# Decay and rate products of an RWKV-7 head pair issued as three groups with alternating row halves instead of eight single products

## The chip, the cores and the metric

One core of a Trainium2 chip runs the whole kernel. The metric is device time in microseconds, the median over runs of the whole program. Engines: PE (TensorE, matmul), DVE (VectorE), ACT (ScalarE), POOL (GpSimd), SP (SyncE, DMA issue). Matmul results land in PSUM, which has eight banks; one bank holds 512 fp32 columns of 128 partitions. All matmuls here are fp32, and each shows as two instructions in the trace.

## The reference, cut to what matters

The model has two layers over 768 tokens (256 context, 512 latent) with model width 1024. Each layer holds a bidirectional RWKV-7 time mixing, a conformer convolution, a gated MLP, a merge and a SwiGLU. The change lies in the first. Per layer, for each of the two directions d, the reference computes

```python
lw = (w0[d] + jnp.tanh(z[..., ow:ow + DECAY_LORA]) @ w_up[d])      # DECAY_LORA = 64
decay = jnp.exp(-jnp.exp(-jax.nn.softplus(-lw) - 0.5))
a = jax.nn.sigmoid(a0[d] + z[..., oa:oa + ICLR_LORA] @ a_up[d])    # ICLR_LORA = 64
k_d = kf * (1.0 + (a - 1.0) * k_a)
S = S * w_t - (S kk_t) kka_t^T + v_t k_t^T                         # the scan over tokens, per head
```

with `kk = k * k_k`, divided by its norm over each head (the norm squared is floored). The two products with `w_up[d]` and `a_up[d]` contract over 64, half of PE's 128 rows.

## The kernel before

**Staging.** `pair_phase(l)` handles layer l in turns t = 0 to 9; turns 0 to 7 each start one pair of heads (KT = 8 pairs, 128 of the 1024 channels each). In turn t PE issues `dense(t)`, the projections of pair t, woven with `scan(t-1)`, the chunked delta rule of the pair before, and with side work. The order is written by hand: `WEAVE["PE", l, t]` is a string in which d takes the next step of `dense`, s the next of `scan` and x the next of the side work. Strings ("A", l, t) and ("V", l, t) do the same for ACT and DVE, where p is a step of the pair's preparation (`rest`). Semaphores between engines are wrapped as events; each `wait_ge` holds up everything behind it on its engine.

**The scan of a pair** has, among other work, 16 bursts of 48 matmuls in 32x32 tiles per turn (96 instructions in the trace, L1156). Between bursts DVE masks a product (L2617, event t_masked), subtracts one (L2622, u_taken) and transposes it (L2601, x_turned); the next burst of that chain waits for it. Two chains, h0 and h1, alternate. Below, um3h0 is the burst that yields chain h0's u-product at level 3, um3h1 the same of chain h1, and tm4h0 the next burst of chain h0, whose product DVE masks for level 4. In layer 0 with t = 3 they start at 615.54, 619.45 and 622.08 us in the profile.

**The dense part.** k, r and v of a pair each take 8 accumulating matmuls per half of the tokens (`k_tiles`, `r_tiles`, `v_tiles`; L1040): the latent half (512 columns) lands in bank 0, the context half (256 columns) in bank 1. Between them stand single products (`single()`, L1052): four decay products and four rate products (64 rows deep; direction 0 in the upper 64 rows, direction 1 in the lower), and the two norm sums of kk², `norm_tile(t, 0)` and `norm_tile(t, 1)`, 128 rows deep. Both norm sums land in bank 0 (`LANDS["kkn"]`). Before any product starts in a bank, `hold` makes PE wait for the reader of the bank's last tenant:

```python
def hold(b, reader):
    if b in held:
        pe.wait_ge(*held[b])
    held[b] = reader
```

The reader of a k or r result is ACT's copy (L1806, L1807; raw_k, raw_r), of a decay product ACT's sigmoid `decay_gate` (L1858), of a rate product `rate_gate` (L1869), and of a norm sum DVE's `norm_max` (L2446, kk_max). DVE's queue of a turn has, in `rest`, the token shifts of k and r (L2394, L2398), two scans over 768 tokens (L2491) that wait for all four decay gates, a subtraction (L2495), then `norm_max(0)` and `norm_max(1)`.

**Tables.** `tables(n)` on ACT loads the function table n if another is loaded (ACT_TABLE_LOAD, L1701).

## Time and profile before

| what | before |
|---|---|
| median of 3 runs | 4074.63 us (4072.68 to 4075.27) |
| profiled execution, its own time | 4079.55 us |
| its span in the profile | 4077.7 us |
| PE busy | 3880.4 us, 95% |
| DVE busy | 1687.0 us, 41% |
| ACT busy | 1146.1 us, 28% |
| POOL busy | 551.5 us, 14% |
| mean granted clock of PE | 0.986 |

The span is the profile's stretch from first to last instruction. The profiled execution is one more run, 4.9 us longer than the median of the three. Busy shares are means over stages with different limits.

### The profile page before, as it was taken

To read this page: it belongs to the slowest core of one execution; us is meant where nothing else is said; L and a number is where in the kernel's file an instruction comes from. 1 tells how busy PE (TensorE), PEld (TensorE's weight loads), DVE (VectorE), ACT (ScalarE), POOL (GpSimd) and SP (SyncE) were. 2 spreads that over 40 slices of the span, in tenths; PEclk is the share of its full clock that TensorE was granted. 3 is DMA by queue.
4 is the path that set the end of the run, shared out by engine and by line. 5 is a ranking of instruction groups with operands and counts; after the bars stand their busy time and mean duration, and the time that the engine had idled before them with its cause. 6 is when DMAs were issued, how large, how long until landed. Compare 5 with 4: busy or idle time off the path is not lost.

```text
span 4077.7 us, 111806 instructions
## 1 busy us (share of the span) xinstructions
PE 3880.4 (95%) x51352; PEld 2546.8 (62%) x51352; DVE 1687.0 (41%) x2721; ACT 1146.1 (28%) x2003; POOL 551.5 (14%) x436
## 2 busy tenths in 40 slices
PE   7899999999999999999999988999998999999998
PEld 3566666666555555655555556666666556678887
DVE  2555566664862111322231254555555422122232
ACT  3444444442122000200000344444444221021001
POOL 0000000000032221122232000000000023213443
PEclk8999999999999999999999999999999999999999
DMA  5000000000333223211112300000010253242224
GB/s 205 25 9 24 25 25 25 25 22 28 108 131 104 93 88 95 79 61 62 52 62 73 123 25 9 23 23 23 23 34 21 68 194 114 83 144 92 85 89 129
DMA packets 76337, 277.40 MB, mean 68 GB/s; under 512 B 8672, under 2 KB 13024, under 8 KB 75488
## 3 DMA queue, kind: packets, MB, share of 16 engines
q1 hardware_dynamic: 67968, 235.96, 18.1%
q10 hardware_dynamic: 6624, 29.04, 1.9%
q8 instruction: 408, 6.68, 0.7%
q0 software_dynamic: 1280, 5.24, 0.3%
q14 instruction: 57, 0.47, 0.0%
HBM read 256.58 MB, written 13.63 MB: 66 GB/s over the span
## 4 chain that ended last, share of the span: by engine, by line
PE 90%; ACT 4%; issue 3%; DVE 2%; DMA 1%; POOL 0%; ACTq 0%; DVEq 0%; SPq 0%; POOLq 0%
PE psum L1156 17%; PE psum L1670 16%; PE psum L1040 12%; PE psum L741 11%; PE psum L1467 9%; PE psum L1602 6%; PE psum L1052 5%; PE psum L1562 3%; PE psum L1625 2%; PE psum L1188 2%; PE psum L732 2%; PE psum L1000 2%; DMA ring<-w_stream_in 1%; PE psum L1018 1%; PE psum L921 1%
## 5 line engine op out<-in xcount | busy, mean ns | idle before, releaser
L1156 PEld LDWEIGHTS psum<-arena 32*32 32x32 f32 (+3 forms) x40512 | 697.6, 117 | 375.4 <-issue 301.4
L1156 PE MATMUL psum<-arena 32*32 32x32 f32 (+4 forms) x40512 | 790.8, 208 | 105.4 <-issue 73.7
L1040 PE MATMUL psum<-arena,ring 128*128 128x512 f32 (+1 forms) x1408 | 573.1, 523 | 2.5 <-ACT arena L1858 1.6
L741 PE MATMUL psum<-arena,ring 128*128 128x512 f32 (+1 forms) x1264 | 463.1, 524 | 3.8 <-DVE arena L2552 3.8
L741 PEld LDWEIGHTS psum<-arena,ring 128*128 128x128 f32 x1264 | 238.8, 191 | 230.3 <-issue 200.7
L1670 PE MATMUL psum<-arena 128*128 128x384 f32 (+1 forms) x1344 | 368.6, 433 | 0.0
L1040 PEld LDWEIGHTS psum<-arena,ring 128*128 128x128 f32 x1408 | 239.2, 191 | 142.0 <-issue 115.5
L1670 PEld LDWEIGHTS psum<-arena 128*128 128x128 f32 x1344 | 255.4, 190 | 106.4
L2991 POOL DMA_DIRECT2D ya_spill<-arena x16 | 8.8, 550 | 1995.2 <-DVE arena L2552 1995.2
L1670 PE MATMUL psum<-arena,ring 128*128 128x384 f32 (+1 forms) x1008 | 278.5, 433 | 0.0
L1670 PEld LDWEIGHTS psum<-arena,ring 128*128 128x128 f32 x1008 | 191.6, 190 | 79.5
L2834 DVE TENSOR_TENSOR arena<-psum,arena 128x384 f32<-128x384 f32 (+1 forms) x210 | 99.2, 489 | 309.9 <-PE psum L1670 309.9
L1467 PE MATMUL psum<-arena 128*128 128x384 f32 (+1 forms) x768 | 215.9, 434 | 3.0 <-POOL arena L3028 1.8
L1701 ACT ACT_TABLE_LOAD x106 | 136.0, 1283 | 191.2 <-PE psum L1052 83.2
L1467 PEld LDWEIGHTS psum<-arena 128*128 128x128 f32 x768 | 145.9, 191 | 66.6 <-issue 4.0
L1467 PE MATMUL psum<-arena,ring 128*128 128x384 f32 (+1 forms) x576 | 169.1, 437 | 14.5 <-DMA ring<-w_stream_in 8.2
L2376 DVE TENSOR_TENSOR arena<-arena 128x768 f32<-128x768 f32 x192 | 175.2, 930 | 11.5 <-ACT arena L1930 6.6
L2359 DVE SCALAR_TENSOR_TENSOR arena<-arena,par 128x255 f32<-128x255 f32 (+18 forms) x296 | 166.3, 596 | 5.3
L2723 DVE TENSOR_TENSOR arena<-psum,arena 128x384 f32<-128x384 f32 (+1 forms) x120 | 56.6, 488 | 252.0 <-PE psum L1467 251.9
L1467 PEld LDWEIGHTS psum<-arena,ring 128*128 128x128 f32 x576 | 108.3, 191 | 67.9 <-issue 6.5
L1052 PE MATMUL psum<-arena 64*128 64x512 f32 (+3 forms) x304 | 140.9, 544 | 7.1 <-ACT arena L1807 2.3
L1602 PE MATMUL psum<-arena 128*128 128x384 f32 (+1 forms) x528 | 145.1, 433 | 0.0
(175 smaller groups left out, 4428.6 us busy)
## 6 DMA issues: line engine op xcount, KB each, us to landing
ring<-w_stream_in SPq DMA_DIRECT2D x440, 512.0 KB, 3.8
x_spill<-arena ACTq DMA_DIRECT2D x2, 3072.0 KB, 8.7
arena<-x_spill ACTq DMA_DIRECT2D x16, 384.0 KB, 6.5
arena<-ya_spill ACTq DMA_DIRECT2D x6, 768.0 KB, 6.0
ring<-w_stream_in ACTq DMA_DIRECT2D x8, 512.0 KB, 6.4
arena<-x_in ACTq DMA_DIRECT2D x1, 3072.0 KB, 14.3
arena<-ups_in SPq DMA_DIRECT2D x16, 192.0 KB, 2.4
ya_spill<-arena POOLq DMA_DIRECT2D x8, 384.0 KB, 6.3
```

The costliest lines, as they stand in the source:

```text
L741: mm = eng.matmul(psum[0:lhs[k].shape[-1], tile, a - off:b - off], lhsT=lhs[k], rhs=rhs[k][:, a:b], start=(k == 0), stop=(k == len(lhs) - ...
L1040: mm = pe.matmul(bank(j, z=b - a), lhsT=w[k], rhs=hs[k][:, a:b], start=(k == 0), stop=(k == KT - 1))
L1052: pe.matmul(bank(b, z=z - a), lhsT=lhs, rhs=rhs[:, a:z], start=True, stop=True).then_inc(ev.sem, 2 if skip else 1)
L1156: return pe.matmul(out, lhsT=lhs, rhs=rhs, start=start, stop=stop, skip_group_check=True)
L1467: mm = pe.matmul(bank(FREE_BANK[i], z=m), lhsT=left[:, k * P:k * P + P], rhs=right[:, k], start=(k == 0 and i != 2), stop=(k == 3), skip_g ...
L1562: mm = pe.matmul(psum[:, tile, a - c0:b - c0], lhsT=w, rhs=mov[k][:, a:b], start=(k == 0), stop=(k == len(mov) - 1), skip_group_check=True)
L1602: mm = pe.matmul(bank(DOWN_BANK[i], z=m), lhsT=left[:, k * P:k * P + P], rhs=right[:, k], start=((p, i) not in begun and k == 0), stop=(c ...
L1670: mm = pe.matmul(bank(b, z=m), lhsT=left[:, k * P:k * P + P], rhs=right[:, k], start=(k == 0 and i != 2), stop=(k == 3), skip_group_check= ...
L1701: act.add_instruction(mybir.InstLoadActFuncSet(name=nc.get_next_instruction_name(), engine=act.engine, act_func_set_id=n))
L2359: return dve.scalar_tensor_tensor(out=out, in0=in0, scalar=w, in1=out, op0=ALU.mult, op1=ALU.add)
L2376: dve.tensor_tensor(out, a, b, ALU.mult).then_inc(ev.sem, 1)
L2834: dve.tensor_tensor(out, x, y, op).then_inc(*V.mark(name))
```

## The change

1. The eight single decay and rate products of a turn become three groups (`up_group`), each of eight matmuls with 64 rows and 128 columns that take direction 0 (upper rows) and direction 1 (lower rows) by turns, into bank 0 for direction 0 and bank 1 for direction 1 (in turn 0 banks 2 to 7). Group "first" is decay of the latent half, "both" is decay and rate of the context half, "last" is rate of the latent half. In `dense`, "first" follows the k tiles, "both" the latent r tiles, "last" the context r tiles. Each is one letter of the weave.
2. Both norm products move earlier among the context r tiles, and the weave strings of turns 1 to 7 are rewritten.
3. ACT's order in `rest` follows; on DVE `r_shift(0)` moves ahead of the two scans; one weave string of DVE changes by one letter.
4. Everywhere `tables(...)` is called ahead of the wait instead of behind it.

```diff
-UP_ORDER = ((0, 0), (1, 1), (1, 0), (0, 1))
+UP_ORDER = dict(lw=((0, 0), (1, 0), (1, 1), (0, 1)), la=((1, 1), (0, 1), (0, 0), (1, 0)))
+UP_GROUPS = dict(first=(("lw", 0, 0),), both=(("lw", 1, 0), ("la", 1, 256)), last=(("la", 0, 0),))
+UP_BANK = dict(first=2, both=4, last=6)
-LANDS = dict(mean=(1, 1), bonus=(1, 0), lw=(0, 0, 0, 1), la=(1, 1, 0, 0), kkn=(0, 0), var=(1, 1), gu=(0, 0))
+LANDS = dict(mean=(1, 1), bonus=(1, 0), kkn=(0, 0), var=(1, 1), gu=(0, 0))
...
+        def up_bank(t, group, d):
+            return d + (0 if t else UP_BANK[group])
...
-                def up_tile(t, name, ev, src, n, reader, j):
-                    if t < KT:
-                        g = KT * l + t
-                        d, half = UP_ORDER[j]
...
-                        yield from single(name, ev, g, j, half, ups_block(g, n, side(d)), slot(src)[side(d)], reader.at(g, j), True)
...
+                def up_group(t, group):
...
+                    name, half, at = UP_GROUPS[group][-1]
+                    for d in DIRS:
+                        hold(up_bank(t, group, d), (sw if name == "lw" else sa).at(g, UP_ORDER[name].index((d, half))))
+                    for name, half, at in UP_GROUPS[group]:
...
+                        for c in range(a, b, P):
+                            for d, h in UP_ORDER[name]:
+                                if h != half:
+                                    continue
+                                mm = pe.matmul(bank(up_bank(t, group, d), a=at + c - a, z=at + c - a + P), lhsT=ups_block(g, n, side(d)),
+                                               rhs=slot(src, c, c + P)[side(d)], start=True, stop=True, skip_group_check=True)
+                                if c + P == b:
+                                    mm.then_inc(ev.sem, 1)
+                    yield
...
-                    yield from decay_tile(t, 0)
                     yield from k_tiles(t, 1, 4, 6)
-                    yield from decay_tile(t, 1)
                     yield from k_tiles(t, 1, 6, 8)
-                    yield from decay_tile(t, 2)
+                    yield from up_group(t, "first")
                     yield from r_tiles(t, 0, 0, 2)
-                    yield from decay_tile(t, 3)
                     yield from r_tiles(t, 0, 2, 4)
-                    yield from rate_tile(t, 0)
                     yield from r_tiles(t, 0, 4, 6)
-                    yield from rate_tile(t, 1)
                     yield from r_tiles(t, 0, 6, 8)
+                    yield from up_group(t, "both")
                     yield from r_tiles(t, 1, 0, 2)
-                    yield from rate_tile(t, 2)
-                    yield from r_tiles(t, 1, 2, 4)
-                    yield from rate_tile(t, 3)
                     yield from norm_tile(t, 0)
-                    yield from r_tiles(t, 1, 4, 6)
+                    yield from r_tiles(t, 1, 2, 6)
                     yield from norm_tile(t, 1)
                     yield from r_tiles(t, 1, 6, 8)
+                    yield from up_group(t, "last")
...
                     yield from k_shift(1)
+                    yield from r_shift(0)
                     if prep:
                         for d in DIRS:
                             dve.wait_ge(*sw.at(g, 3))
...
-                    yield from r_shift(0)
                     yield from norm_max(0)
```

In PE's queue of layer 0, turn t=3, before, the stretch from the burst of chain h1 at level 3 to the second norm product reads as follows. L1156 rows are bursts, L1040 rows are r tiles, L1052 with 64 rows deep are rate products, and the two L1052 rows that wait for kk_square are the norm products.

```order
653 L1156 MATMUL psum<-arena 32x32 [waits x_turned]
654 L1156 MATMUL psum<-arena 32x32 x47
655 L1040 MATMUL psum<-arena,ring 128x256 x2
656 L1052 MATMUL psum<-arena 128x256 [waits rate_gate,ups_in_0]
657 L1156 MATMUL psum<-arena 32x32 [waits x_turned]
658 L1156 MATMUL psum<-arena 32x32 x47
659 L1052 MATMUL psum<-arena,const 128x512 [waits rate_gate,kk_square]
660 L1040 MATMUL psum<-arena,ring 128x256 x2
661 L1156 MATMUL psum<-arena 32x32 [waits t_masked]
662 L1156 MATMUL psum<-arena 32x32 x47
663 L1052 MATMUL psum<-arena,const 128x256 [waits kk_max,kk_square]
```

After the change the same engine and place, with the line numbers of the new program (L1173 bursts, L1054 r tiles, L1066 norm products, L1122 the groups; row 642 opens the group "last").

```order
631 L1066 MATMUL psum<-arena,const 128x512 [waits rate_gate,kk_square]
632 L1054 MATMUL psum<-arena,ring 128x256 x2
633 L1173 MATMUL psum<-arena 32x32 [waits x_turned]
634 L1173 MATMUL psum<-arena 32x32 x47
635 L1054 MATMUL psum<-arena,ring 128x256 x2
636 L1066 MATMUL psum<-arena,const 128x256 [waits kk_max,kk_square]
637 L1173 MATMUL psum<-arena 32x32 [waits x_turned]
638 L1173 MATMUL psum<-arena 32x32 x47
639 L1054 MATMUL psum<-arena,ring 128x256 x2
640 L1173 MATMUL psum<-arena 32x32 [waits t_masked]
641 L1173 MATMUL psum<-arena 32x32 x47
642 L1122 MATMUL psum<-arena 128x128 [waits raw_r,kk_max,ups_in_0]
```

The first norm product moved from behind both x_turned bursts to ahead of them, and the second from behind the next t_masked burst to ahead of the second x_turned burst; it still waits for kk_max, the read of the first.

In DVE's queue the same turn, before, from the subtraction for chain h0 to the read of the first norm sum, reads:

```order
254 L2622 TENSOR_TENSOR arena<-arena,psum 128x384 [waits u_product]
255 L2601 STREAM_TRANSPOSE arena<-arena 128x384 [waits u_taken]
256 L2491 SCALAR_TENSOR_TENSOR arena<-arena 128x768 [waits decay_gate] x2
257 L2622 TENSOR_TENSOR arena<-arena,psum 128x384 [waits u_product]
258 L2495 TENSOR_TENSOR arena<-arena 128x768 [waits decay_sums]
259 L2601 STREAM_TRANSPOSE arena<-arena 128x384 [waits u_taken]
260 L2617 TENSOR_TENSOR arena<-psum,const 128x384 [waits t_product]
261 L2394 SCALAR_TENSOR_TENSOR arena<-arena,par 128x511 [waits raw_r]
262 L2398 SCALAR_TENSOR_TENSOR arena<-arena,par 128x511 [waits shifted_r]
263 L2446 TENSOR_SCALAR arena<-psum 128x512 [waits kk_norm]
```

After, the same stretch, up to the first norm sum's read (L2463):

```order
254 L2639 TENSOR_TENSOR arena<-arena,psum 128x384 [waits u_product]
255 L2618 STREAM_TRANSPOSE arena<-arena 128x384 [waits u_taken]
256 L2411 SCALAR_TENSOR_TENSOR arena<-arena,par 128x511 [waits raw_r]
257 L2415 SCALAR_TENSOR_TENSOR arena<-arena,par 128x511 [waits shifted_r]
258 L2639 TENSOR_TENSOR arena<-arena,psum 128x384 [waits u_product]
259 L2509 SCALAR_TENSOR_TENSOR arena<-arena 128x768 [waits decay_gate]
260 L2618 STREAM_TRANSPOSE arena<-arena 128x384 [waits u_taken]
261 L2634 TENSOR_TENSOR arena<-psum,const 128x384 [waits t_product]
262 L2509 SCALAR_TENSOR_TENSOR arena<-arena 128x768 [waits decay_gate]
263 L2513 TENSOR_TENSOR arena<-arena 128x768 [waits decay_sums]
264 L2463 TENSOR_SCALAR arena<-psum 128x512 [waits kk_norm]
```

The two shifts of r (L2394 and L2398, now L2411 and L2415) moved from just ahead of `norm_max(0)` to ahead of the scans, and the two scans are apart by a transpose and a mask; the number of instructions between the subtraction and `norm_max(0)` is the same.

In layer 1 there are no context r tiles. PE's queue of its turn t=3 before, around the norm products (L1188 are transposes by matmul):

```order
3910 L1156 MATMUL psum<-arena 32x32 [waits x_turned]
3911 L1156 MATMUL psum<-arena 32x32 x47
3912 L1052 MATMUL psum<-arena 128x256 [waits rate_gate,ups_in_1]
3913 L1052 MATMUL psum<-arena,const 128x512 [waits rate_gate,kk_square]
3914 L1156 MATMUL psum<-arena 32x32 [waits t_masked]
3915 L1156 MATMUL psum<-arena 32x32 x47
3916 L1188 MATMUL psum<-const,arena 128x128 [waits token_major]
3917 L1188 MATMUL psum<-const,arena 128x128 x3
3918 L1052 MATMUL psum<-arena,const 128x256 [waits kk_max,kk_square]
```

And after, from the group "both" to the second norm product and the burst behind it:

```order
3835 L1122 MATMUL psum<-arena 128x128 [waits decay_gate,raw_r,ups_in_1]
3836 L1122 MATMUL psum<-arena 128x128 x7
3837 L1173 MATMUL psum<-arena 32x32 [waits t_masked]
3838 L1173 MATMUL psum<-arena 32x32 x47
3839 L1205 MATMUL psum<-const,arena 128x128 [waits token_major]
3840 L1205 MATMUL psum<-const,arena 128x128 x3
3841 L1066 MATMUL psum<-arena,const 128x512 [waits rate_gate,kk_square]
3842 L1173 MATMUL psum<-arena 32x32 [waits x_turned]
3843 L1173 MATMUL psum<-arena 32x32 x47
3844 L1066 MATMUL psum<-arena,const 128x256 [waits kk_max,kk_square]
3845 L1173 MATMUL psum<-arena 32x32 [waits x_turned]
3846 L1173 MATMUL psum<-arena 32x32 x47
```

Between the first and the second norm product stands one burst; before there were a burst and four transposes, and the first came two bursts later in the scan.

## Rows read from the trace of the kernel before

**Rows 1.** The page: busy time, the chain that ended last, and the costliest PE group.

```profile
PE 3880.4 (95%) x51352; PEld 2546.8 (62%) x51352; DVE 1687.0 (41%) x2721; ACT 1146.1 (28%) x2003; POOL 551.5 (14%) x436
...
PE 90%; ACT 4%; issue 3%; DVE 2%; DMA 1%; POOL 0%; ACTq 0%; DVEq 0%; SPq 0%; POOLq 0%
...
L1156 PE MATMUL psum<-arena 32*32 32x32 f32 (+4 forms) x40512 | 790.8, 208 | 105.4 <-issue 73.7
```

**Rows 2.** Timeline, PE, turn t=3 of layer 0: start us, length us, engine, line, operation.

```profile
595.38 1.12 PE L1052 MATMUL psum<-arena 64*128 64x512 f32 x2
596.43 0.70 PE L1040 MATMUL psum<-arena,ring 128*128 128x256 f32 x2
...
598.88 0.70 PE L1052 MATMUL psum<-arena 64*128 64x256 f32 x2
599.51 1.13 PE L1040 MATMUL psum<-arena,ring 128*128 128x256 f32 x4
```

**Rows 3.** Timeline, PE: a run of `product()` in the same row halves.

```profile
357.75 2.06 PE L1156 MATMUL psum<-arena 64*128 64x128 f32 x32
359.74 0.44 PE L1188 MATMUL psum<-const,arena 128*128 128x128 f32 x2
```

**Rows 4.** Timeline, DVE, turn t=3 of layer 0, from the product of um3h0 on.

```profile
617.24 0.55 DVE L2622 TENSOR_TENSOR arena<-arena,psum 128x384 f32<-128x384 f32 x1 [3.10 <-PE psum L1156]
...
624.63 0.75 DVE L2398 SCALAR_TENSOR_TENSOR arena<-arena,par 128x511 f32<-128x511 f32 x1
626.83 0.69 DVE L2446 TENSOR_SCALAR arena<-psum 128x512 f32<-128x512 f32 x1 [1.45 <-PE psum L1052]
```

**Rows 5.** Timeline, PE, the same stretch.

```profile
617.10 2.42 PE L1040 MATMUL psum<-arena,ring 128*128 128x512 f32 x6
...
622.08 1.02 PE L1156 MATMUL psum<-arena 32*32 32x32 f32 x96
623.03 1.13 PE L1040 MATMUL psum<-arena,ring 128*128 128x256 f32 x4
624.09 0.70 PE L1052 MATMUL psum<-arena 64*128 64x256 f32 x2
...
625.67 1.13 PE L1052 MATMUL psum<-arena,const 128*128 128x512 f32 x2
626.63 1.03 PE L1040 MATMUL psum<-arena,ring 128*128 128x256 f32 x4
627.59 1.26 PE L1156 MATMUL psum<-arena 32*32 32x32 f32 x96
```

**Rows 6.** Timeline, DVE, turn t=3 of layer 1.

```profile
2735.30 0.56 DVE L2622 TENSOR_TENSOR arena<-arena,psum 128x384 f32<-128x384 f32 x1 [2.00 <-PE psum L1156]
...
2741.86 0.75 DVE L2398 SCALAR_TENSOR_TENSOR arena<-arena,par 128x511 f32<-128x511 f32 x1
2744.04 0.69 DVE L2446 TENSOR_SCALAR arena<-psum 128x512 f32<-128x512 f32 x1 [1.44 <-PE psum L1052]
```

**Rows 7.** Timeline, ACT: a rate gate of 256 columns.

```profile
615.65 0.47 ACT L1869 ACTIVATE arena<-psum,par 128x256 f32<-128x256 f32 x1 [3.40 <-PE psum L1052]
```

**Rows 8.** Timeline, ACT: a table load in a norm between phases.

```profile
2284.87 1.28 ACT L1701 ACT_TABLE_LOAD   x1 [1.24 <-PE psum L944]
```

**Rows 9.** Timeline, PE: two idle stretches inside bursts.

```profile
392.37 0.44 PE L1156 MATMUL psum<-arena 32*32 32x32 f32 x28 [1.53 <-issue]
...
3142.23 0.39 PE L1156 MATMUL psum<-arena 32*32 32x32 f32 x25 [3.08 <-issue]
```

**Rows 10.** Windows: us, length, busy PE, PEld, DVE, ACT, POOL, granted clock, DMA share, GB/s.

```profile
376.00:488.00 112.00, 107.98 (x2746) 72.88 (x2745) 64.92 (x100) 51.26 (x92) 0.55 (x1) 0.97 0.07 23
596.00:702.00 106.00, 104.06 (x2744) 71.28 (x2743) 64.55 (x100) 51.25 (x92) 0.54 (x1) 1.00 0.08 24
...
392.90:399.70 6.80, 6.80 (x105) 3.32 (x106) 1.08 (x2) 0.69 (x1) 0.00 (x0) 0.50 0.02 5
3142.20:3149.20 7.00, 4.87 (x256) 3.10 (x255) 2.61 (x5) 0.00 (x0) 0.00 (x0) 1.00 0.02 5
```

More of the change, by code:

```diff
@@ L186 @@
 WEAVE.update((("PE", 1, t), (
-    "ddddxsdxxssxsddxdssxdxxdddddddssdddsxdxsdsxdddddssdddsddsdssdsdssdsddxddsdsxddddsddssssssddsdssssssd"
-    "sssssssdssssssssssssssssssssssssss")) for t in (1,))
+    "ddddxsdxxssxsddxdssxdxxddddddddsxsdxsddsddsxddsddsdsdssssdssdsddxddsdsxddddsddssssssddsdssssssdsssss"
+    "ssdssssssssssssssssssssssssss")) for t in (1,))
 WEAVE.update((("PE", 1, t), (
-    "xxsssdsxssxxdxxddddsxdsdxsddddsdddsdddsdddxsdsddsddsddsddsddsxdsddsxdsdsddxsddddsddsdsssddssdsssssds"
-    "ssdssssdddsssssssssssssssssssssssssss")) for t in range(2, KT))
+    "xxsssdsxssxxdxxddddsxdsdxsddddsddddsddsdxsddsddsddsddxsdsxdsdssdsdsddxsddddsddsdsssddssdsssssdsssdss"
+    "ssdddsssssssssssssssssssssssssss")) for t in range(2, KT))
 WEAVE.update((("PE", 1, t), (
@@ L645, in state_sum, with up_result @@
             return bank((6 if n < 8 else 4) + d, rows, n % 8 * C, n % 8 * C + C)
+        def up_bank(t, group, d):
+            return d + (0 if t else UP_BANK[group])
+        def up_result(t, name, j):
+            d, half = UP_ORDER[name][j]
+            group, at = [(k, at) for k, parts in UP_GROUPS.items() for n, h, at in parts if (n, h) == (name, half)][0]
+            a, b = HALVES[half]
+            return bank(up_bank(t, group, d), a=at, z=at + b - a)
         def wk(c, rows=slice(0, P), a=0, b=P):
@@ L1087, in bonus_tile @@
                         yield from single("bonus", bonus, g, j, j, heads, slot(BN + g % 2), bv.at(g, j), False)
-                def up_tile(t, name, ev, src, n, reader, j):
-                    if t < KT:
-                        g = KT * l + t
-                        d, half = UP_ORDER[j]
-                        pe.wait_ge(ups[g % 3], 16 * (g // 3 + 1))
-                        if t == 0 and j == 0:
-                            pe.wait_ge(*phases["lora"]["A"].end(l))
-                            pe.wait_ge(*phases["lora"]["V"].end(l))
-                        yield from single(name, ev, g, j, half, ups_block(g, n, side(d)), slot(src)[side(d)], reader.at(g, j), True)
-                def decay_tile(t, j):
-                    yield from up_tile(t, "lw", lw, LW, 0, sw, j)
-                def rate_tile(t, j):
-                    yield from up_tile(t, "la", la, LA, 1, sa, j)
+                def up_group(t, group):
+                    if t >= KT:
+                        return
+                    g = KT * l + t
+                    pe.wait_ge(ups[g % 3], 16 * (g // 3 + 1))
+                    if t == 0 and group == "first":
+                        pe.wait_ge(*phases["lora"]["A"].end(l))
+                        pe.wait_ge(*phases["lora"]["V"].end(l))
+                    name, half, at = UP_GROUPS[group][-1]
+                    for d in DIRS:
+                        hold(up_bank(t, group, d), (sw if name == "lw" else sa).at(g, UP_ORDER[name].index((d, half))))
+                    for name, half, at in UP_GROUPS[group]:
+                        (a, b), n, src, ev = HALVES[half], "lw la".split().index(name), LW if name == "lw" else LA, lw if name == "lw" else la
+                        for c in range(a, b, P):
[7 more added lines that the diff above has]
+                    yield
                 def norm_tile(t, j):
@@ L1854, in decay_gate @@
                                 act.wait_ge(*kq.at(g - 1, 1))
-                            d, half = UP_ORDER[j]
-                            act.wait_ge(*lw.at(g, j))
+                            d, half = UP_ORDER["lw"][j]
                             tables(SIGMOID)
-                            act.activation(slot(SW + d, *HALVES[half]), landed("lw", j, half), ACT.Sigmoid, bias=vec(f"w0{d}", t)).then_inc(sw.sem, 1)
+                            act.wait_ge(*(lw.at(g, j) if half == 0 else la.at(g, j - 2)))
+                            act.activation(slot(SW + d, *HALVES[half]), up_result(t, "lw", j), ACT.Sigmoid, bias=vec(f"w0{d}", t)).then_inc(sw.sem, 1)
                             yield
@@ L1865, in rate_gate @@
                                 act.wait_ge(*sv.at(g - 1, 3))
-                            d, half = UP_ORDER[j]
+                            d, half = UP_ORDER["la"][j]
+                            tables(SIGMOID)
                             act.wait_ge(*la.at(g, j))
-                            tables(SIGMOID)
-                            act.activation(slot(SA + d, *HALVES[half]), landed("la", j, half), ACT.Sigmoid, bias=vec(f"a0{d}", t)).then_inc(sa.sem, 1)
+                            act.activation(slot(SA + d, *HALVES[half]), up_result(t, "la", j), ACT.Sigmoid, bias=vec(f"a0{d}", t)).then_inc(sa.sem, 1)
                             yield
```

52 lines of the change are left out of this document (26 added, 26 removed).

## Prediction

> **What bounds the kernel now.** I read the page first: PE is busy 95% of the span and is 90% of the chain that ended last [rows 1]. So a microsecond of PE work removed is a microsecond of time, as long as PE does not wait where it did not before; DVE and ACT count only through what they make PE wait for. Next I read the timeline of a whole turn of a pair phase on PE and DVE. In it PE goes from burst to product to burst with no idle time but a few stretches that the profile puts down to issue, while DVE waits for PE: the burst before the subtraction at 617.24 was waited for 3.10 us, and the first norm sum 1.45 us [rows 4]. So DVE has 1.45 us in hand at the norm sum, by PE's present order. Last I read the windows for the granted clock.
>
> **What the change removes.** A single product costs from its start to the start of the next instruction 1.05 us with 512 columns (595.38 to 596.43) and 0.63 us with 256 (598.88 to 599.51) [rows 2]. A turn has four of each: 4 x 1.05 + 4 x 0.63 = 6.7 us, and 16 turns 107.5 us.
>
> **What it adds.** 24 matmuls of 64 rows and 128 columns per turn in three groups of eight, 16 instructions in the trace each. The trace shows this shape, in alternating row halves and different banks, in another place: 32 instructions from 357.75 to 359.74, 1.99 us, the drain at both ends included [rows 3]. A group is half of that, 1.0 us; three are 3.0 us, and 16 turns 48 us. If the fixed part of those 1.99 us is a larger share than I can see, a group may take 1.15 us, which makes 7 us more. The columns done side by side are what halves the time: the single products take 1.05 us for two passes of 512 columns, the groups as many columns of both directions at once. The work of the removal minus this is **-60 us** (107.5 - 48 = 59.5).
>
> **Norm products: the new wait.** The second norm product lands in the bank of the first and so waits for `norm_max(0)`, which is behind the same ten DVE instructions as before (the order listings: subtraction, transpose, two shifts, subtraction, scan, transpose, mask, scan, subtraction). PE, however, comes there much sooner.
>
> Layer 0. DVE works without a gap from 617.24 to 624.63 + 0.75 = 625.38, which is 8.14 us; with `norm_max`'s 0.69 that is 8.83 us, from 0.14 us after the end of PE's burst um3h0 at 617.10 [rows 4, 5]: 8.97 us. The order within does not change this sum, and the decay gates for which the scans wait come in time: "both" ends one burst ahead of this point, and four gates of 256 columns, 0.47 us each [rows 7], fit into the subtraction, transpose, shifts and subtraction. PE in the new order has between um3h0's end and the second norm product: two r tiles (1.06, as 623.03 to 624.09), burst um3h1 (0.95, as 622.08 to 623.03), the first norm product (0.96, 625.67 to 626.63), two r tiles (0.96), a burst (0.95), two r tiles (0.96) [rows 5]: 5.84 us. So PE stands for 8.97 - 5.84 = 3.1 us, a little less with what the first tile waits for a rate gate; I take 3.0. Behind it in PE's queue are the burst tm4h1 and everything else, so all of it is lost.
>
> Layer 1 has no r tiles of the context half. From um3h1's product DVE works from 2735.30 to 2741.86 + 0.75 = 2742.61, with `norm_max` 8.0 us [rows 6]. PE has four transposes (0.5), norm product and burst (1.9) and, because "both" is nearer here, some 0.55 us of waiting for the rate gates, together 3.0 us. PE stands 5.0 us.
>
> In turn 0 there is no scan work on DVE between, and I count half. Sum: 7.5 x 3.0 + 7.5 x 5.0 = **+60 us**. Bounds: 45 if PE loses 1 us a turn elsewhere on its way there, 70 if turn 0 waits like the others (64) and the handoffs add 0.4 us a turn (6).
>
> **Smaller waits.** After "both" four gates of 256 columns follow on ACT, 0.47 us each [rows 7]; the first tile into bank 1 needs two of them, 0.2 + 2 x 0.45 = 1.1 us, and PE brings one burst, 0.95 us: 0.15 us a turn. The group "last" waits for `norm_max(1)`, which DVE reaches one mask after the burst behind the first; PE has 1 us to spare there. Turn 0, without bursts, has more. I take **+6 us**, between 2 and 12.
>
> **Tables.** A load is ahead of the wait now. At 2284.87 ACT is idle 1.24 us and then loads for 1.28 us [rows 8], in a norm on the path between phases; there the load disappears into the idle time. The end of the kernel has the same chain once more. 2 x 1.24 = **-2.5 us**. In the pair phases the loads stand in idle time of ACT, which is busy 28% [rows 1]; nothing, and if ACT were late there the load would only be earlier.
>
> **The clock.** The turn t=1 of layer 0 takes 112 us at a mean clock of 0.97, turn t=3 106 us at 1.00, with the same number of instructions [rows 10]. In the first is a stretch of 6.8 us at 0.50, the lower level, 1.2 GHz, right behind an idle stretch of PE of 1.53 us; behind one of 3.08 us at 3142.23 the clock stays at 1.00 [rows 9, 10]. A stretch of 6.8 us at half clock costs up to 3.4 us. The new waits make 16 idle stretches of 3 to 5 us where there were none. Of two such rows one lost its clock; I take half, 8 stretches, and 2 us each, since shorter ones cost less: **+16 us**, between 0 and 16 x 3.4 = 54.
>
> The Trainium skill ("TensorE: Matmul & The Clock Gate", Part 1 on the clock gate) has PE's clock go back to the lower level when PE has stood idle, and advises against idle gaps on it. The row at 392.37 agrees with that, the one at 3142.23 does not. By the rule each of the 16 new waits is a candidate; that is the third rival below, and it speaks against the change.
>
> **Sum.** -60 + 60 + 6 - 2.5 + 16 = +19.5 us on the profiled execution's 4079.55, that is 4099. It is 4.9 us above the median of the runs; on the median, 4074.63 + 19.5 = **4094 us**.
>
> **Rivals.**
> *The waits eat the saving and the clock holds.* As in 3142.23's case. Then +3.5 us: 4078. For it: half of the rows shown. It needs both sums to be right, so the band within 0.2% (8 us, about what a measurement of this kernel can tell from no change) gets a chance of 0.14.
> *Faster: the wait lies over idle time that is there anyway.* PE has 73.7 us of idle time in its scan matmuls put down to issue [rows 1], a lack of instructions in bursts that follow one another closely. While PE stands at the norm product its queue can fill, and the bursts behind it run without such stretches. If a third of it goes, -25 us, and the clock holds: 4074.6 + 3.5 - 25 = 4053 us. It decides from -12 us on. Against it: the three removed tiles bring bursts nearer to one another elsewhere, which makes more of these stretches. Chance 0.22, 4050 to 4066.
> *The clock drops at every wait, layer 0's too.* 16 x 3.4 = 54 in place of 16: up to 4132; with 2 to 2.5 us each, 4110 to 4118. Chance 0.15.
> *The row halves don't run side by side.* Then a group takes what its instructions take one by one, 2 us, and the saving falls to 12 us: 4142 us. The run at [rows 3] speaks against it: 62 ns an instruction. Chance 0.03.
> The forecast itself, 4083 to 4110, has 0.46.
>
> **How the numbers follow.** Faster by more than 0.2%: 0.22. Within: 0.14. Slower: 0.46 + 0.15 + 0.03, with rounding 0.64. The range reaches from the upper part of the faster rival to the clock case: 4058 to 4116; below it I leave 0.1, above 0.1. The likeliest case alone: 4083 to 4110.
>
> **What the profile after would show.** Three groups of 16 instructions per turn at 1.0 us from start to next start; PE idle 3 us before the norm product with 256 columns in layer 0 and 5 us in layer 1, released by DVE's `norm_max`, about 60 us in all in the row of the norm products; `norm_max(0)` on DVE with no idle time before it, where it has 1.45 us now; ACT's two loads between phases inside idle time; more stretches with clock 0.5 behind the norm product. I would be wrong if PE reached the norm product later than I count (if bursts on the way wait for DVE, the wait only moves), if DVE did the ten instructions in a shorter time because it waits for nothing else, or if issue stretches change by more than 10 us.

## The result and the profile after

The changed kernel takes 4137.07 us (median of 4 runs, 4127.57 to 4147.18), the kernel before 4073.65 us in the same comparison (4067.53 to 4075.27). The ratio is 1.015, 95% interval 1.0132 to 1.0168: slower by some 63 us. The sign was forecast, the size (19.5 us) was not, and the time lies above the range.

The page after has these lines for those of [rows 1]: busy time of each engine, then the chain that ended last.

```profile
PE 3861.0 (93%) x51864; PEld 2595.7 (63%) x51864; DVE 1685.6 (41%) x2721; ACT 1136.4 (28%) x2003; POOL 552.4 (13%) x436
...
PE 85%; DVE 7%; ACT 4%; issue 3%; DMA 1%; POOL 0%; ACTq 0%; DVEq 0%; SPq 0%; POOLq 0%
```

PE does 19.4 us less by its busy time, in a span that is 54.2 us longer (4131.9 to 4077.7 us): its idle time went from 197.3 to 270.9 us. DVE now has 7% of the chain, where it had 2%; that share is a rough sign, since it is 4% in the kernel before with the table loads alone moved (e4 below) and 5% in a version that has none of these waits (e11). The mean granted clock fell from 0.986 to 0.971.

The groups of PE by line, after, say where it stands idle (busy us, mean ns | idle us before the group, and what ended it):

```profile
L1173 PE MATMUL psum<-arena 32*32 32x32 f32 (+4 forms) x40512 | 807.4, 211 | 101.2 <-issue 69.3 <-ACT arena L2056 9.5 <-ACT arena L2063 3.7
...
L1205 PE MATMUL psum<-const,arena 128*128 128x128 f32 x752 | 114.2, 282 | 22.1 <-ACT arena L2005 20.7 <-ACT arena L1997 1.3
...
L1066 PE MATMUL psum<-arena,const 128*128 128x512 f32 (+1 forms) x208 | 102.9, 580 | 62.0 <-DVE arena L2463 60.4 <-ACT arena L1908 1.0 <-ACT arena L1886 0.5
...
L1122 PE MATMUL psum<-arena 64*128 64x128 f32 x768 | 69.7, 331 | 10.4 <-issue 10.3
```

The norm products wait 60.4 us for `norm_max`, the transposes 20.7 us for a copy on ACT, and the groups 10.3 us for issue. The bursts' idle time put down to issue is 69.3 us, where it was 73.7 [rows 1]. All these together, less what went (a rate gate's 5.2 us and the single products' 7.1 us of before), are the 74 us by which idle time grew.

The timeline of PE in layer 0, turn t=4, answers to [rows 5]:

```profile
507.51 1.13 PE L1054 MATMUL psum<-arena,ring 128*128 128x256 f32 x4
508.57 0.62 PE L1173 MATMUL psum<-arena 32*32 32x32 f32 x48
509.75 0.61 PE L1173 MATMUL psum<-arena 32*32 32x32 f32 x48 [0.56 <-issue]
510.29 1.12 PE L1066 MATMUL psum<-arena,const 128*128 128x512 f32 x2
511.25 1.03 PE L1054 MATMUL psum<-arena,ring 128*128 128x256 f32 x4
512.21 0.84 PE L1173 MATMUL psum<-arena 32*32 32x32 f32 x74
513.60 0.38 PE L1173 MATMUL psum<-arena 32*32 32x32 f32 x22 [0.55 <-issue]
513.91 1.13 PE L1054 MATMUL psum<-arena,ring 128*128 128x256 f32 x4
518.00 1.19 PE L1066 MATMUL psum<-arena,const 128*128 128x256 f32 x2 [2.96 <-DVE arena L2463]
519.13 1.50 PE L1173 MATMUL psum<-arena 32*32 32x32 f32 x96
...
524.00 1.16 PE L1122 MATMUL psum<-arena 64*128 64x128 f32 x16
525.09 1.09 PE L1173 MATMUL psum<-arena 32*32 32x32 f32 x76
```

PE does the two r tiles from 513.91 on and then stands 2.96 us, until 518.00. DVE's rows of the same place answer to [rows 4]. `norm_max` itself no longer waits, where it had waited 1.45 us; but DVE stands 0.94 us ahead of the mask (L2634), until PE's burst at 512.21 is done.

```profile
510.41 0.55 DVE L2639 TENSOR_TENSOR arena<-arena,psum 128x384 f32<-128x384 f32 x1 [0.23 <-PE psum L1173]
...
514.04 0.56 DVE L2634 TENSOR_TENSOR arena<-psum,const 128x384 f32<-128x384 f32 x1 [0.94 <-PE psum L1173]
...
516.30 0.96 DVE L2513 TENSOR_TENSOR arena<-arena 128x768 f32<-128x768 f32 x1
517.18 0.68 DVE L2463 TENSOR_SCALAR arena<-psum 128x512 f32<-128x512 f32 x1
```

Layer 1, turn t=5, PE:

```profile
2876.45 1.98 PE L1054 MATMUL psum<-arena,ring 128*128 128x512 f32 x4
2881.89 0.63 PE L1205 MATMUL psum<-const,arena 128*128 128x128 f32 x4 [3.46 <-ACT arena L2005]
2882.45 1.41 PE L1173 MATMUL psum<-arena 32*32 32x32 f32 x96
...
2887.76 1.10 PE L1066 MATMUL psum<-arena,const 128*128 128x512 f32 x2 [0.26 <-ACT arena L1886]
2888.78 1.02 PE L1173 MATMUL psum<-arena 32*32 32x32 f32 x96
2894.81 1.19 PE L1066 MATMUL psum<-arena,const 128*128 128x256 f32 x2 [5.01 <-DVE arena L2463]
```

Two waits: 5.01 us at the norm product, as forecast, and 3.46 us before the transposes (L1205), which the prediction does not have. ACT's rows show what it did there:

```profile
2878.53 0.60 ACT L1823 ACTIVATE arena<-psum 128x512 f32<-128x512 f32 x1 [12.89 <-PE psum L1054]
...
2879.59 0.93 ACT L1908 ACTIVATE arena<-arena,par 128x768 f32<-128x768 f32 x1
2880.55 0.59 ACT L2002 ACTIVATE arena<-psum 64x512 f32<-64x512 f32 x1
2881.16 0.59 ACT L2005 ACTIVATE arena<-psum 64x512 f32<-64x512 f32 x1
```

The copy of the latent r result (L1823) waits for PE's r tiles; behind it and the square (L1908) stand the copies of the transposed operands (L2002, L2005), and PE's next transposes need the bank that L2005 reads. So PE waits for a copy that could have run many microseconds earlier.

The windows at two of the waits at the norm product, the first of them in layer 0 and the second in layer 1 (length, busy PE, PEld, DVE, ACT, POOL, granted clock, DMA share, GB/s):

```profile
517.20:524.00 6.80, 6.00 (x198) 4.42 (x198) 1.55 (x4) 0.75 (x2) 0.00 (x0) 0.50 0.02 5
2892.90:2903.10 10.20, 7.24 (x306) 6.29 (x306) 3.66 (x7) 1.25 (x3) 0.00 (x0) 0.50 0.01 3
```

The clock is at its lower level, 1.2 GHz, for 6.8 us in the first and 10.2 us in the second. Both stretches begin while PE still waits. In layer 0 the burst at 519.13 takes 1.43 us to the next start in place of 0.95.

### The profile page after: what moved, and what is told of

It reads as the page before. It is cut to its first block, busy times and chain, and to the rows that moved or that the text cites. A ratio compares the mean times of both kernels' runs of the same rounds, so it can differ in the third digit from the quotient of the medians.

```text
span 4131.9 us, 112746 instructions
## 1 busy us (share of the span) xinstructions
PE 3861.0 (93%) x51864; PEld 2595.7 (63%) x51864; DVE 1685.6 (41%) x2721; ACT 1136.4 (28%) x2003; POOL 552.4 (13%) x436
## 4 chain that ended last, share of the span: by engine, by line
PE 85%; DVE 7%; ACT 4%; issue 3%; DMA 1%; POOL 0%; ACTq 0%; DVEq 0%; SPq 0%; POOLq 0%
PE psum L1173 17%; PE psum L1687 15%; PE psum L1054 11%; PE psum L755 9%; PE psum L1484 9%; PE psum L1619 6%; PE psum L1579 3%; DVE arena L2376 3%; PE psum L1066 3%; PE psum L1642 2%; PE psum L1205 2%; PE psum L1014 2%; PE psum L746 2%; PE psum L1122 2%; PE psum L1032 1%
## 5 line engine op out<-in xcount | busy, mean ns | idle before, releaser
L1173 PEld LDWEIGHTS psum<-arena 32*32 32x32 f32 (+3 forms) x40512 | 715.0, 121 | 352.6 <-issue 270.5
L1173 PE MATMUL psum<-arena 32*32 32x32 f32 (+4 forms) x40512 | 807.4, 211 | 101.2 <-issue 69.3
L1054 PE MATMUL psum<-arena,ring 128*128 128x512 f32 (+1 forms) x1408 | 570.1, 528 | 2.5 <-ACT arena L1824 1.3
L755 PEld LDWEIGHTS psum<-arena,ring 128*128 128x128 f32 x1264 | 238.8, 191 | 230.4 <-issue 200.9
L1687 PE MATMUL psum<-arena 128*128 128x384 f32 (+1 forms) x1344 | 368.6, 432 | 0.0
L1054 PEld LDWEIGHTS psum<-arena,ring 128*128 128x128 f32 x1408 | 246.9, 194 | 132.4 <-issue 105.1
L1687 PEld LDWEIGHTS psum<-arena,ring 128*128 128x128 f32 x1008 | 191.5, 190 | 79.6
L1484 PE MATMUL psum<-arena 128*128 128x384 f32 (+1 forms) x768 | 216.0, 435 | 2.7 <-POOL arena L3045 1.8
L1484 PE MATMUL psum<-arena,ring 128*128 128x384 f32 (+1 forms) x576 | 170.0, 439 | 13.7 <-DVE arena L2735 3.9
L2639 DVE TENSOR_TENSOR arena<-arena,psum 128x384 f32<-128x384 f32 x128 | 70.7, 552 | 227.3 <-PE psum L1173 226.6
L1066 PE MATMUL psum<-arena,const 128*128 128x512 f32 (+1 forms) x208 | 102.9, 580 | 62.0 <-DVE arena L2463 60.4
L1823 ACT ACTIVATE arena<-psum 128x512 f32<-128x512 f32 (+1 forms) x88 | 43.8, 497 | 412.0 <-PE psum L1054 412.0
L1484 PEld LDWEIGHTS psum<-arena,ring 128*128 128x128 f32 x576 | 109.1, 192 | 67.4 <-issue 6.5
```

Source lines behind the costliest of these rows:

```text
L755: mm = eng.matmul(psum[0:lhs[k].shape[-1], tile, a - off:b - off], lhsT=lhs[k], rhs=rhs[k][:, a:b], start=(k == 0), stop=(k == len(lhs) - ...
L1054: mm = pe.matmul(bank(j, z=b - a), lhsT=w[k], rhs=hs[k][:, a:b], start=(k == 0), stop=(k == KT - 1))
L1066: pe.matmul(bank(b, z=z - a), lhsT=lhs, rhs=rhs[:, a:z], start=True, stop=True).then_inc(ev.sem, 2 if skip else 1)
L1173: return pe.matmul(out, lhsT=lhs, rhs=rhs, start=start, stop=stop, skip_group_check=True)
L1484: mm = pe.matmul(bank(FREE_BANK[i], z=m), lhsT=left[:, k * P:k * P + P], rhs=right[:, k], start=(k == 0 and i != 2), stop=(k == 3), skip_g ...
L1687: mm = pe.matmul(bank(b, z=m), lhsT=left[:, k * P:k * P + P], rhs=right[:, k], start=(k == 0 and i != 2), stop=(k == 3), skip_group_check= ...
```

## The experiments

Each run has a kernel before beside it on the same chip; "half clock" is 2 x (1 - mean clock) x span, from the mean clock of all its runs: the time that PE spent at the lower level. The two profiles of one and the same kernel, e5 and e11, differ by 3.8 us in the bursts' issue time and their half-clock times by 12 us, so smaller differences tell nothing.

| kernel | median us | ratio to before, 95% interval | half clock us | PE waits for norm_max us |
|---|---|---|---|---|
| before | 4067 to 4074 | 1 | 105 to 111 | 0.9 |
| changed | 4137.07 | 1.0150 (1.0132 to 1.0168) | 257 | 60.4 |
| e1 norm reads early, t >= 2 | 4085.56 | 1.0027 (1.0014 to 1.0040) | 198 | 15.4 |
| e2 copy early | 4102.96 | 1.0076 (1.0060 to 1.0092) | 238 | 58.0 |
| e3 both | 4052.79 | 0.9950 (0.9935 to 0.9965) | 160 | 14.3 |
| e4 before, tables alone | 4070.89 | 0.9993 (0.9983 to 1.0002) | 112 | 0.9 |
| e5 e3, t = 0 and 1 too | 4033.91 | 0.9911 (0.9890 to 0.9932) | 141 | 1.1 |
| e6 before, 3 delays | 4088.52 | 1.0052 (1.0035 to 1.0069) | 129 | 3.3 |
| e7 before, 6 delays | 4135.81 | 1.0165 (1.0144 to 1.0186) | 190 | 0.9 |
| e8 e3, halves in a row | 4067.72 | 1.0005 (0.9995 to 1.0016) | 205 | 13.9 |
| e9 e5, read between scans | 4047.70 | 0.9935 (0.9915 to 0.9955) | 155 | 14.7 |
| e10 e5, reads late | 4090.48 | 1.0051 (1.0034 to 1.0068) | 216 | 46.8 |
| e11 e5 again | 4037.91 | 0.9921 (0.9900 to 0.9941) | 153 | 1.6 |

**e1: the reads of the norm sums earlier on DVE.**

```diff
                     yield from r_shift(0)
+                    if t >= 2:
+                        yield from norm_max(0)
...
                             yield
+                            if d == 0 and t >= 2:
+                                yield from norm_max(1)
...
-                    yield from norm_max(0)
-                    yield from norm_max(1)
+                    if t < 2:
+                        yield from norm_max(0)
+                        yield from norm_max(1)
```

> The changed kernel, with the reads of the two norm sums on DVE moved up in turns 2 to 7 of both layers: norm_max(0) ahead of the first scan, norm_max(1) between the scans. PE's second norm product then finds the read done. In the changed kernel PE stands there 60.4 us in all, about 48 us of it in these turns. Theory A (each such wait also costs clock behind it): the 48 us go, and with them most of the half-clock time behind the waits, 25 to 35 us more; about 4060 us. Rival B (the half-clock stretches are not tied to these waits): 48 us alone, about 4090 us, and the profile has as many half-clock stretches as the changed kernel. Rival C (the wait only moves to the group last, which needs norm_max(1)): under 20 us, 4117 us or more.

It is 51.5 us faster than the changed kernel. The time alone is nearer to B's 4090 than to A's 4060. But the wait fell by 45.0 us and the half-clock time by 59 us, so B's assumption falls: half-clock stretches go with the waits. A's total was too large, in part because something came back; the groups of PE in e1:

```profile
L1173 PE MATMUL psum<-arena 32*32 32x32 f32 (+4 forms) x40512 | 800.3, 209 | 113.5 <-issue 78.6 <-ACT arena L2056 11.8 <-ACT arena L2063 3.8
...
L1066 PE MATMUL psum<-arena,const 128*128 128x512 f32 (+1 forms) x208 | 97.2, 550 | 16.9 <-DVE arena L2463 15.4 <-ACT arena L1908 1.0 <-ACT arena L1886 0.3
```

The bursts' issue time is 78.6 us, against 69.3 in the changed kernel: about 9 us more, which fits idle time that the waits had covered. C falls.

**e2: the copy of the transposed operands earlier on ACT** (layer 1, t >= 2).

```diff
-"xxsssxxxsssssxxxpppppppxpxpppppxxpssspxpspppsspssssssppsppspssssssssssps"
+"xxsssxxxsssssxxxpppppxpppxpppppxxpssspxpspppsspssssssppsppspssssssssssps"
```

> The changed kernel, with one letter of ACT's order in layer 1, turns 2 to 7, moved: the copy of the transposed operands (L2002, L2005) stands ahead of the copy of the latent r result instead of behind it and the square. PE's transposes wait 3.46 us there in each of the six turns, 20.7 us. Theory A: these 20.7 us go, and some 10 us of half-clock cost with them; about 4107 us. Rival B (no clock in it): 4116 us. Rival D (PE comes sooner to the norm product and stands there longer instead): no change, 4137 us.

34 us faster than the changed kernel, a little beyond A. The wait of turn t=5 is gone, as the timeline of PE around the same transposes shows, and no other took its place:

```profile
2851.44 1.98 PE L1054 MATMUL psum<-arena,ring 128*128 128x512 f32 x4
2853.26 0.60 PE L1205 MATMUL psum<-const,arena 128*128 128x128 f32 x4
2853.79 1.02 PE L1173 MATMUL psum<-arena 32*32 32x32 f32 x96
```

The 34 us are not all wait and clock: the wait is 20.7 us, the half-clock time falls by 19 us, which is some 7 us of time, and the bursts' issue time falls too, from 69.3 to 60.7 us. That last is against what e1 showed, and no run explains it.

**e3: both.**

> Both edits of the two runs before this one together. Theory A: the waits cost 48 + 21 us and the clock 35 to 45 us, so the time falls to about 4030 us, below the kernel before the change by some 40 us, since the groups' saving of 60 us then stands nearly alone. Rival B: the clock is not tied to the waits, about 4068 us, the same as before the change. Rival C: 4100 us or more.

4052.8 us, 84 us faster than the changed kernel, where e1 and e2 alone sum to 86: the two edits add up. It is 0.5% below the kernel before. The time lies between A's 4030 and B's 4068; the half-clock time is 97 us below the changed kernel's, so the clock is tied to the waits, and A is again some 20 us too hopeful, in part for the same reason (the bursts' issue time is 83.6 us now).

**e4: the tables alone.** The kernel before with `tables(...)` ahead of the waits.

> The kernel before the change with only the table loads moved ahead of the waits. Theory: 2.5 us less from two norms between phases, 4071 us, not to be told from no change. Rival: loads now stand ahead of work that was ready, or change ACT's instruction supply, so that it is slower by more than 5 us.

4070.9 us against 4072.5, no difference that can be told.

**e5: the same for turns 0 and 1.** `norm_max(0)` ahead of the scans in every turn, `norm_max(1)` between them in turn 0 too.

> The kernel of e3 with the read of the first norm sum moved up in turns 0 and 1 as well (the second's too in turn 0). e3 still shows 14.3 us of PE waiting for these reads, all in turns 0 and 1. Theory A: 10 to 14 us of idle time go and a few us of clock with them: 4036 us, 0.9% below the kernel before the change. Rival: in turn 1 the second read, left behind the scans, makes the group last wait in place of the norm product, so less than 5 us.

4033.9 us and, once more as e11, 4037.9: 0.8 to 0.9% below the kernel before. This version beats both, and the time is A's.

**e6 and e7: waits without groups.** The kernel before, with k = 3 and k = 6.

```diff
                         total = by_chunk(slot(SW + 1))[:, :, C - 1:C].to_broadcast([P, NCH, C])
+                        for n in range(k):
+                            dve.tensor_tensor(by_chunk(slot(kr(g, 0, 0))), total, by_chunk(slot(SW + 1)), ALU.subtract).then_inc(again.sem, 1)
+                            dve.wait_ge(*again.at(g, n))
```

> The kernel before the change, with DVE's subtraction ahead of norm_max(0) (0.95 us) issued three times more in each turn 0 to 7, each repetition writing the same values. PE had 2.1 to 2.7 us in hand at the second norm product, so it stands 0.5 to 1.2 us a turn, 10 to 15 us in all. Both theories: 4083 to 4092 us. It is the base of e7.

> As e6 with six repetitions: PE now stands 3.5 to 4.5 us a turn at the second norm product, as in the changed kernel, with no group and no other edit. Idle time there about 60 us, some 50 more than in e6. Theory A (a wait of this length in every turn costs clock behind it): e7 is 70 us or more above e6, and the half-clock time rises by 60 us or more. Rival B (the lost clock of the changed kernel comes from the groups or from the new order of bursts): e7 is 45 to 55 us above e6 and the half-clock time of the pair phases stays within 20 us of e6's.

e6's time is in the range given, but its waits are elsewhere than I said, and it is 21 us above the kernel before beside it, more than the 10 to 15 us expected: at the norm product PE stands only 3.3 us, and in the bursts 8.3 us for DVE's transpose (L2605) and 5.0 us for its mask (L2621), which stand behind the delays too. e7 is 47 us above e6. That is in B's range of 45 to 55 and well below A's 70; but the half-clock time rose by 61 us, as A has it and against B's 20. Neither theory held whole, and here too PE waits in the bursts. The bursts of e6 and e7:

```profile
L1157 PE MATMUL psum<-arena 32*32 32x32 f32 (+4 forms) x40512 | 790.3, 208 | 106.2 <-issue 61.3 <-ACT arena L2040 11.5 <-DVE arena L2605 8.3
```

```profile
L1157 PE MATMUL psum<-arena 32*32 32x32 f32 (+4 forms) x40512 | 792.7, 209 | 135.3 <-issue 47.4 <-DVE arena L2605 27.8 <-DVE arena L2621 27.5
```

From e6 to e7 the transpose's wait grows by 19.5 us (8.3 to 27.8) and the mask's by 22.5 (5.0 to 27.5), the half-clock time by 61 us, and the issue time falls by 14 us (61.3 to 47.4). So waits on PE cost clock in a kernel without groups, too, and issue time falls beside them, which both of my theories had left out.

**e8: one direction after the other within a group.**

```diff
-                        for c in range(a, b, P):
-                            for d, h in UP_ORDER[name]:
-                                if h != half:
-                                    continue
+                        for d, h in UP_ORDER[name]:
+                            if h != half:
+                                continue
+                            for c in range(a, b, P):
```

> The kernel of e3, with each group's matmuls in another order: all of direction 0, then all of direction 1, instead of by turns. Theory A (the saving comes from row halves that run side by side): an instruction then takes 0.107 us instead of 0.062, 16 of them 1.7 us instead of 1.0, and 48 groups 34 us more: 4085 us (less, since in the group both the halves still change every two matmuls). Rival (the order within a group does not matter, the saving is one of fewer mode changes and smaller tiles): within 5 us of e3, 4053 us.

15 us above e3 by the medians, 22 by the ratios (the two ran on different chips): between the rival's 5 and A's 34, which had made no allowance for the group "both". The timeline of PE shows the groups "first" and "both" in e8, and "first"-sized ones in e3 below it, each with what starts behind:

```profile
593.12 1.68 PE L1122 MATMUL psum<-arena 64*128 64x128 f32 x16
594.74 1.02 PE L1173 MATMUL psum<-arena 32*32 32x32 f32 x96
...
609.02 1.26 PE L1122 MATMUL psum<-arena 64*128 64x128 f32 x16
610.21 1.02 PE L1173 MATMUL psum<-arena 32*32 32x32 f32 x96
```

```profile
604.23 1.16 PE L1122 MATMUL psum<-arena 64*128 64x128 f32 x16
605.33 1.02 PE L1173 MATMUL psum<-arena 32*32 32x32 f32 x96
```

In a row a group takes 1.62 us (1.19 for "both", whose halves still change every two matmuls), by turns 1.10. That is 16 x (1.62 + 1.19 + 1.62 - 3.30) = 18 us over the kernel. The row halves do run side by side: instruction by instruction, the trace of e3 has the matmuls of the two halves starting in pairs 4 to 7 ns apart, a pair every 0.11 us, where in e8 one half alone starts an instruction every 0.11 us. This is a third of the groups' saving of 107.5 - 53 = 54.5 us. The Trainium skill ("TensorEngine Tiling (Array Packing)", Key Properties) says that different tiles of the array can load and multiply at the same time; these rows agree. The half-clock time rose too, by 45 us, with the same waits; why, no run tells.

**e9 to e11: one place, three lengths of wait.** e5, with the read of the first norm sum in turns 2 to 7 between the scans (e9), or both reads behind them as in the changed kernel (e10), and e5 itself.

> The kernel of e5, but in turns 2 to 7 the read of the first norm sum stands between the two scans on DVE. PE then stands 0.6 us (layer 0) and 2.5 us (layer 1) a turn at the second norm product, about 19 us in all. Theory A, with the price of a wait that e1 and e3 showed (about 1.2 us of time for each us of wait): 20 to 28 us above e5; in layer 0 hardly a half-clock stretch behind so short a wait, in layer 1 most turns have one. Rival (short waits cost only their length, or are taken back by fewer issue stretches): 8 to 19 us.

> The kernel of e5, but in turns 2 to 7 both reads stand behind the scans and the subtraction, as in the changed kernel: waits of 3 and 5 us, 45 to 48 us in all. Theory A: 55 to 75 us above e5, and 50 to 80 us more half-clock time in the pair phases. Rival: 45 us or less above e5.

> The kernel of e5 again, beside e9 and e10 on the same chip, as the base of both. 0.8 to 1.0% below the kernel before the change, as in e5.

Against e11 the wait is 13.1 us longer in e9 and the time 9.8 us; in e10 45.2 and 52.6 us. e9 is the rival's case (8 to 19 us), and with runs of 4035 to 4050 against 4034 to 4046 us it can hardly be told from e11 at all. e10 lies between the two theories, just under A's 55 and above the rival's 45. The groups of PE in e11 and e10:

```profile
L1173 PE MATMUL psum<-arena 32*32 32x32 f32 (+4 forms) x40512 | 797.7, 209 | 113.3 <-issue 80.0 <-ACT arena L2056 10.6 <-ACT arena L2063 3.7
...
L1066 PE MATMUL psum<-arena,const 128*128 128x512 f32 (+1 forms) x208 | 95.6, 542 | 4.2 <-DVE arena L2463 1.6 <-ACT arena L1886 1.3 <-ACT arena L1908 1.0
```

```profile
L1173 PE MATMUL psum<-arena 32*32 32x32 f32 (+4 forms) x40512 | 804.0, 211 | 101.2 <-issue 69.5 <-ACT arena L2056 10.8 <-ACT arena L2063 3.7
...
L1066 PE MATMUL psum<-arena,const 128*128 128x512 f32 (+1 forms) x208 | 101.4, 572 | 49.1 <-DVE arena L2463 46.8 <-ACT arena L1886 1.3 <-ACT arena L1908 1.0
```

In e9 the half-clock time in all is that of e11 (155 to 153 us). That does not mean that the clock holds through short waits: e11 has, without such waits, idle stretches in its bursts that the profile puts down to issue, and half-clock stretches behind them, in the same turns of layer 1. One of them, from e11's timeline, with the window behind it (columns as in the windows above):

```profile
2818.04 1.16 PE L1173 MATMUL psum<-arena 32*32 32x32 f32 x103 [2.21 <-issue]
...
2818.90:2825.70 6.80, 6.36 (x160) 4.40 (x147) 3.16 (x6) 4.36 (x6) 0.00 (x0) 0.50 0.03 5
```

In e9 short waits stand in turns where e11 has these. In e10 it is 63 us more. At most half of that is lost, and PE is busy in about three quarters of it (in all half-clock stretches of the changed kernel's profile, 187.1 of 244.4 us), so about 24 us; 45 of wait and 24 of clock, less some 11 of issue time (80.0 to 69.5 in the bursts), is 58 us against 52.6 measured.

## Why the prediction was wrong

Two terms of the sum failed. The clock was put at +16 us and cost about 55. The smaller waits were put at +6 us, and a wait for ACT of 20.7 us, which the prediction does not have at all, was behind them. The sign was right, and so were the work saved and the size of the norm products' wait, the last in part by luck.

**What bounds the kernel.** Right: PE, and its waits.

**The saving, -60 us.** Right, and on the low side. A group takes 1.10 us, not 1.0: 1.1 x 48 = 53 us for 48. But PE's work fell by more than the 55 us that this leaves. Its busy time fell 19.4 us, while its busy time at the lower clock rose from 87.6 us in the profile before to 187.1 us. If the same work takes twice as long there, that is about 50 us of lengthening, and the work fell by about 69 us. This is an estimate, and no run isolates where the further 14 us come from; that bursts and tiles change places less often is possible and not shown.

**The norm products, +60 us.** 60.4 us, but not by the working. In layer 0 with t=4 both sides were longer than counted. PE came to the second norm product 7.53 us after the end of um3h0 (507.51 to 515.04) and not 5.84, with 1.1 us of idle stretches inside two bursts. DVE needed 10.35 us (507.51 to 517.86) and not 8.97, with 0.94 us of it spent waiting for PE's burst, which the count as gapless work leaves out. The two errors cancel nearly, and the wait is 2.96 us. Nor are the turns alike: turn 0, counted half, waits 3.37 us in layer 0 and 5.09 in layer 1, the most or nearly; turn 1, counted whole, 1.96 and 3.15; turns 2 to 7 wait 2.94 to 2.98 us in layer 0 and 4.00 to 5.49 in layer 1. The mechanism is right, as e1, e5 and e10 show by moving the read alone; that the sum is right to the microsecond is luck. (In the listing of PE's queue before, row 653 is tm4h0, the burst at 622.08, and not a burst of chain h1 as the text above it says; the working uses the right one.)

**Smaller waits, +6 us.** Wrong: 20.7 us came from one place that it does not name. The step took ACT's weave for unchanged, since its strings are, and asked only what the gates would wait for. But the letters of a string say how many steps go first, not which; `rest` had been put in another order, so the sixth and seventh steps ahead of the copy of the transposed operands were now the r copy, which waits for the last r tile, and the square. PE's transposes in six turns of layer 1 stood 3.46 us behind it. Taking the wait out is worth 34 us on the changed kernel (e2) and 33 on e1 (e3). The rate gates' waits stayed small, and the groups have 10.3 us of issue time that the sum does not have.

**Tables, -2.5 us.** e4 shows 1.6 us less, inside what can be told.

**The clock, +16 us.** This is the step that failed most. Half-clock time rose from about 110 to 257 us, at three quarters busy some 55 us of time, over three times the term and right at the upper bound given (54), which was then left out of the range. The rate of one half came from two rows, one with a drop and one without. The trace of before had more to read: in its pair phases are 13 idle stretches of PE of 1.5 us or more inside bursts or at products, all put down to issue. For 8 of them a half-clock stretch begins between the start of the idle time and 2 us behind its end, one lies in a stretch that had begun already, and 4 have none. Two longer waits outside them, of 4.6 and 3.8 us (until 47.94 and 1049.86), both have one, of 6.8 us. So rate and length were both read too low. In the changed kernel all 16 waits at the norm product and all six at the transposes have a half-clock stretch that way, two of them inside one that had begun before. The stretches at the norm product are 3.4 to 10.2 us long in layer 0 and 6.8 to 20.5 us in layer 1; those of e10, where no wait at the transposes is near, are still up to 13.7 us, so it is not the second wait that makes them long. In the thirteen profiles together 76 waits for DVE or ACT in the pair phases are 2.8 us or longer. For 68 of them a half-clock stretch begins that way, five lie in one, and three, all in turn 0 of layer 0, have none.

Not all of the rise belongs to waits. e10 and e11 put the norm waits of turns 2 to 7 at 63 us of half clock, about 24 us of time; e3 and e5 put those of turns 0 and 1 at some 19 us of half clock; e2, and e3 against e1, put the transposes' wait at 19 to 38. About 40 us of half clock, some 15 us of time, stay when all these waits are gone (e11 against the kernel before). There the profile has 22 idle stretches of 1.5 us or more put down to issue in the pair phases, where the kernel before has 13; why the groups' kernel has more of them is open. The Trainium skill ("TensorE: Matmul & The Clock Gate", Part 1) warns of idle gaps for this reason; e10 against e11 agrees. The third rival was this case; its 4110 to 4118 was still too low because the ACT wait was missing.

**Rival: the wait lies over idle time that is there anyway.** It fits three comparisons and not a fourth, and is too small to turn the sign. The issue time of the bursts is 69.3 us with the waits and 78.6 without (e1), 69.5 and 80.0 (e10, e11), 47.4 with the long waits and 61.3 with the short (e7, e6): 9 to 14 us, not 25. But when e2 took the transposes' wait away, it fell to 60.7 us. What was said against this rival came true as well: with most or all of the waits gone the new order has 80 to 84 us of such time (e3, e5, e11), where the kernel before has 74.

The bookkeeping of the profiled executions is -69 of work, +74 of idle time (60 and 21 of waits, 10 of the groups' issue, -17 of waits and issue time that went) and +50 of clock. But for rounding it gives the 54 us of the span, and must, since the work was worked out from the rest. With the +55 from the half-clock time of all runs it is 60, against 63 measured.

## What to carry to other kernels

A product moved earlier in the critical engine's queue brings its bank's last reader into the path; move that reader in the same edit, by adding up what stands before it in its own queue. Two reads on DVE moved in this way, with one letter on ACT, turned this change from 1.5% slower to 0.8 to 0.9% faster. Where an order is written as counts of steps, an unchanged string over reordered steps is a changed order, and the listing of every engine has to be read for it, not only of those where the diff has a string. A wait on PE of some 3 us or more should be priced above its length: here 1.14 us of time for each us of wait (e1), 1.16 (e10 against e11) and 1.19 (e7 against e6), of clock lost less issue time that went, and 1.5 where the wait at the transposes goes (e2; e3 against e1; the small change at the norm product counted in). And before a rate is read off two rows, all rows of the kind are to be counted: the trace of before had 13.

## What the runs showed of the hardware

In layer 1 of e9 and e11 PE has 31 idle stretches of 1.5 to 2.5 us, from a wait or put down to issue. For 18 a half-clock stretch begins in them or within 2 us behind, five lie in one, and eight have none. Waits of that length (e9, 13.1 us in all) added none to the sum. Waits of 3 to 5.5 us (e10) add 63 us of half clock in twelve turns, and the half-clock stretches at these waits last up to 13.7 us, although PE works again. The idle time inside bursts that is put down to issue was smaller beside longer waits in three comparisons (e1, e7, e10) and larger in one (e2). Alternating row halves in different banks take 1.10 us for 16 instructions of 64 rows and 128 columns, one half after the other 1.62 us, and the second form came with 45 us more of half clock at equal waits, which is left open.
